# A Fourier branch whose channel transform moves from the tiles to once per unit (8 cores, Trainium2)

## The reference, cut to what matters

```python
def fourier_branch(a, w_fmix, b_fmix):
    a4 = a.reshape(B, S, 4, 128).astype(jnp.float32)
    f = jnp.fft.fft2(a4, axes=(1, 3), norm="ortho").real.astype(a.dtype)
    y = jnp.einsum("bsgc,gcd->bsgd", f, w_fmix) + b_fmix
    return y.reshape(B, S, 512)
...
h = rmsnorm(x, norm_g) * (1.0 + scale[:, None, :]) + shift[:, None, :]
a, ga, u, v, gb, ma, mb = jnp.split(h @ w_in, IN_SPLITS, axis=-1)
y_a = fourier_branch(a, w_fmix, b_fmix) * jax.nn.silu(ga)
y_b = sgu_branch(u, v, sgu_ln_g, sgu_ln_b, w_s, b_s) * jax.nn.silu(gb)
merged = jax.nn.sigmoid(ma) * (y_a @ w_pa) + jax.nn.sigmoid(mb) * (y_b @ w_pb)
out = x + gate[:, None, :] * (merged @ w_out)      # then a final rmsnorm
```

## Time and profile before

| | |
|---|---|
| median of 3 timed runs | 1279.31 us (1278.76 to 1287.62) |
| the profiled execution's own time | 1272.01 us |
| its span, slowest core | 1270.5 us (cores 1264.0 to 1270.5) |
| granted TensorE clock, mean | 0.992 to 0.995 of full |
| busy share PE, DVE, ACT, POOL | 96%, 49%, 38%, 28% |

### The profile page before, as it was taken

How to read it: one execution, slowest core, us unless ns; L and a number is a source line. 1 busy time by engine, 2 the same in 40 slices (tenths; PEclk the granted TensorE clock), 3 DMA queues, 4 the chain that set the end, 5 groups by cost and what they waited for, 6 DMA issues and landing times.

```text
span 1270.5 us, 19981 instructions; the slowest of 8 cores (1264.0 to 1270.5 us)
## 1 busy us (share of the span) xinstructions
PE 1222.7 (96%) x6504; PEld 587.9 (46%) x6504; DVE 627.7 (49%) x945; ACT 483.2 (38%) x818; POOL 349.5 (28%) x430
## 2 busy tenths in 40 slices
PE   6798999999999999989999999999999999999997
PEld 1354454444444455545444444444444444444443
DVE  0383265364756578844435434443446444344434
ACT  1483312323423368743332333243323423333322
POOL 0221132730522332203713213213128122132121
PEclk9899999999999999999999999999999999999999
DMA  8999895234426297656312212121262112121111
GB/s 273 265 254 186 167 170 164 67 116 147 156 80 208 77 302 266 194 164 137 100 50 67 84 50 84 67 90 60 84 136 86 72 62 95 50 84 67 64 70 67
DMA packets 57331, 158.21 MB, mean 125 GB/s; under 512 B 6026, under 2 KB 18698, under 8 KB 56078
## 3 DMA queue, kind: packets, MB, share of 16 engines
q1 hardware_dynamic: 46814, 130.58, 31.2%
q0 software_dynamic: 9120, 17.96, 9.2%
q10 hardware_dynamic: 1296, 8.40, 1.9%
HBM read 143.41 MB, written 31.47 MB: 138 GB/s over the span
## 4 chain that ended last, share of the span: by engine, by line
PE 84%; DMA 8%; DVE 2%; POOL 2%; issue 2%; ACT 1%; ACTq 0%; SPq 0%; DVEq 0%; POOLq 0%
PE ps L680 42%; PE ps L607 13%; PE ps L490 6%; PE ps L778 6%; PE ps L772 6%; PE ps L690 5%; PE ps L447 3%; DMA arena<-w_ada 2%; DMA arena<-Gd 2%; DMA arena<-w_out 2%; DMA arena<-xA 1%; POOL arena L783 1%; POOL arena L675 1%; DMA Gd<-arena 1%; PE ps L500 1%
## 5 line engine op out<-in xcount | busy, mean ns | idle before, releaser
L680 PE MATMUL ps<-arena 128*128 128x512 bf16 x2688 | 602.6, 380 | 2.4 <-DVE arena L729 1.7
L680 PEld LDWEIGHTS ps<-arena 128*128 128x128 bf16 x2688 | 262.1, 98 | 318.3 <-issue 8.0
L764 ACT ACTIVATE arena<-ps 128x512 bf16<-128x512 f32 x192 | 113.2, 596 | 282.8 <-PE ps L680 257.6
L783 POOL TENSOR_TENSOR arena<-arena 128x512 bf16<-128x512 bf16 x84 | 116.3, 1384 | 248.5 <-DVE arena L781 248.5
L775 DVE TENSOR_TENSOR arena<-ps,arena 128x512 bf16<-128x512 f32 x96 | 66.3, 691 | 223.1 <-PE ps L772 223.1
L607 PE MATMUL ps<-arena 128*128 128x512 bf16 x768 | 171.3, 379 | 4.0 <-DVE arena L783 1.5
L408 POOL TENSOR_TENSOR stat<-stat,eps_sb 128x1 f32<-128x1 f32 (+1 forms) x114 | 29.2, 256 | 380.9 <-ACT arena L615 298.6
L612 DVE TENSOR_TENSOR arena<-ps,arena 128x512 f32<-128x512 f32 x96 | 66.0, 691 | 126.8 <-PE ps L607 126.8
L607 PEld LDWEIGHTS ps<-arena 128*128 128x128 bf16 x768 | 74.6, 98 | 93.2 <-issue 5.5
L427 DVE TENSOR_SCALAR arena<-arena,stat 128x1024 bf16<-128x1024 f32 x96 | 81.6, 876 | 60.1 <-POOL stat L410 59.8
L421 ACT ACTIVATE arena<-arena 128x1024 bf16<-128x1024 f32 x96 | 101.2, 1054 | 22.9 <-DMA arena<-xA 16.9
(11 more groups left out here) (80 smaller groups left out, 936.9 us busy)
## 6 DMA issues: line engine op xcount, KB each, us to landing
arena<-xB SPq DMA_DIRECT2D x96, 512.0 KB, 4.4
arena<-xA SPq DMA_DIRECT2D x48, 512.0 KB, 6.3
yu<-arena SPq DMA_DIRECT2D x48, 512.0 KB, 2.8
arena<-w_ada SPq DMA_DIRECT2D x24, 512.0 KB, 5.6
arena<-w_in POOLq DMA_DIRECT2D x9, 1024.0 KB, 17.9
arena<-w_ada ACTq DMA_DIRECT2D x8, 1024.0 KB, 23.7
Gd<-arena SPq DMA_DIRECT2D x48, 128.0 KB, 5.0
arena<-Gd SPq DMA_DIRECT2D x12, 512.0 KB, 8.1
```

What stands on the lines that cost most here:

```text
L680: S.pe([lambda e, kc=kc: e.matmul(ps[b][:], lhsT=w_in_sb[:, sec, kc, col:col + 128], rhs=tb.hT[:, kc, :], start=(kc == 0), stop=(kc == 7)) ...
L764: S.op("act", lambda e, b=b, so=so: e.activation(out=bv(so, 512), in_=ps[b][:], func=AF.Sigmoid), reads=[("ps", b)], writes=gk(so, 1024))
L783: S.op("pool" if dmc < 7 else "dve", lambda e: e.tensor_tensor(out=tb.mg[:, dmc, :], in0=tb.mg[:, dmc, :], in1=bv(sl[1], 512), op=ALU.add) ...
```

## The change

`csw` loses its third part (-S). The new `z_tr(uz, g)` multiplies all 1056 columns of the real part of a group with C and of the imaginary part with S, in six matmuls of 352 columns, and evicts each in place, over the spectrum, as bf16, on ScalarE and VectorE in turn. `fourier_gate` takes the place of `fourier_out`: it has no matmul; VectorE forms sum and difference of the two transformed parts in f32 in `O_TYB`, and then adds the bias and multiplies.

The places: for unit 0 the transform is ahead of the pair's `u_section`; tile 0's gates come between the two u sections and tile 1's in the first four steps of tile 0's merge loop. For unit 1 the transform is in tile 4 after the GA section, that tile's gates after its u section. For unit 2 it is in tile 5, a group after each of the four sections. In tiles 2, 3 and 5 to 11 the gates are emitted between the GA section and the u section.

```diff
-            S.op("act", lambda e, g=g, b=b: e.activation(out=csw[:, g, 2, :], in_=ps[b][:, 128:256], func=AF.Copy, scale=-1.0),
...
+    def z_tr(uz, g):
+        for r in range(2):
+            zr = Zv[:, uz, g, r].rearrange("p s w -> p (s w)")
+            for c in range(3):
+                b = newbank()
+                zc = zr[:, c * 352:(c + 1) * 352]
+                S.pe([lambda e, b=b, zc=zc, r=r: e.matmul(ps[b][:, 0:352], lhsT=csw[:, g, r, :], rhs=zc, start=True, stop=True)],
+                     reads=[("z", g, uz), ("csw", g)], writes=[("ps", b)])
+                evict(zc, ps[b][:, 0:352], [("ps", b)], [("zq", g, uz, r, c)])
+
+    def fourier_gate(tb, u, t, g):
         uz = (1, 0, 1)[u]
         s0, s1 = 4 * t, (4 * t + 8) % 16
...
+        tf = fv(O_TYB, 512)
+        tv = tf.rearrange("p (s h w) -> p s h w", s=4, h=2)
+        rk = [("z", g, uz)] + [("zq", g, uz, r, c) for r in range(2) for c in range(3)]
+        for h, sl, w0, op in ((0, s0, 0, ALU.add), (1, s1, 2, ALU.subtract)):
+            S.op("dve", lambda e, h=h, sl=sl, w0=w0, op=op: e.tensor_tensor(
+                out=tv[:, :, h, :], in0=Zv[:, uz, g, 0, sl:sl + 4, w0:w0 + 64], in1=Zv[:, uz, g, 1, sl:sl + 4, w0:w0 + 64], op=op),
+                reads=rk + ["tyf"], writes=[("tyh", h)] + (gk(O_TYB, 2048) if h == 0 else []))
+        v = tb.sga[:, g, :]
+        sk = gk(tb.a + 1024 * g, 1024)
+        S.op("dve", lambda e: e.scalar_tensor_tensor(out=v, in0=tf, scalar=bfm_sb[:, g:g + 1], in1=v, op0=ALU.add, op1=ALU.mult),
+             reads=gk(O_TYB, 2048) + [("tyh", 0), ("tyh", 1), "tab2"] + sk, writes=sk + gk(O_TYB, 2048) + ["tyf"])
...
+    for g in range(4):
+        z_tr(1, g)
+    u_section(T0)
+    for g in range(4):
+        fourier_gate(T0, 0, 0, g)
+    u_section(TB1)
     for tb in pair:
-        u_section(tb)
-    for i, tb in enumerate(pair):
         sgu(tb)
-        fourier_out(tb, 0, i)
...
+        if dmc < 4:
+            fourier_gate(TB1, 0, 1, dmc)
...
         def after(sec):
             finish()
+            if T == 5:
+                z_tr(1, sec)
...
         after(2)
+        if T == 4:
+            for g in range(4):
+                z_tr(0, g)
+        else:
+            for g in range(4):
+                fourier_gate(tb, u, t, g)
         u_section(tb)
         after(3)
+        if T == 4:
+            for g in range(4):
+                fourier_gate(tb, u, t, g)
...
         sgu(tb)
-        fourier_out(tb, u, t)
```

More of the change, by code:

```diff
@@ L203 @@
 O_CSW = O_FG + 4096
-O_F = O_CSW + 3072
+O_F = O_CSW + 2048
 O_WST = O_F + 512
@@ L322, in build_nc @@
     fg_bc = fv(O_FG, 1024)
-    csw = bv(O_CSW, 1536).rearrange("p (g v d) -> p g v d", g=4, v=3)
+    csw = bv(O_CSW, 1024).rearrange("p (g v d) -> p g v d", g=4, v=2)
     F_sb = bv(O_F, 128)
@@ L385, in channel_tables @@
                  reads=["tab2"] + ck, writes=[("ps", b)])
-            S.op("act", lambda e, g=g, b=b: e.activation(out=csw[:, g, 0:2, :].rearrange("p v d -> p (v d)"), in_=ps[b][:, 0:256], func=AF.Copy),
-                 reads=[("ps", b)], writes=[("csw", g)])
-            S.op("act", lambda e, g=g, b=b: e.activation(out=csw[:, g, 2, :], in_=ps[b][:, 128:256], func=AF.Copy, scale=-1.0),
+            S.op("act", lambda e, g=g, b=b: e.activation(out=csw[:, g].rearrange("p v d -> p (v d)"), in_=ps[b][:, 0:256], func=AF.Copy),
                  reads=[("ps", b)], writes=[("csw", g)])
@@ L735, in sgu @@
                  reads=gk(to, 1024) + sk, writes=sk)
-    def fourier_out(tb, u, t):
+    def z_tr(uz, g):
[7 more added lines that the diff above has]
+                evict(zc, ps[b][:, 0:352], [("ps", b)], [("zq", g, uz, r, c)])
```

## The result

| | before | after |
|---|---|---|
| median of all four executions, same chip | 1283.46 us | 1315.36 us |
| the three that the ratio uses | 1278.76 to 1287.62 us | 1310.38 to 1315.61 us |
| ratio of the times | | 1.025, 95% interval 1.0215 to 1.0284 |
| span of core 7 | 1270.5 us | 1303.7 us |
| TensorE matmuls | 6504 | 6384 |

What follows compares the result with a forecast made beforehand. TensorE's queue of matmuls, almost without holes, was taken as the bound. Saved columns and new waits summed to +23.9 us, with +5 for the clock +29: 1308 us against the median of 1279.3, range 1287 to 1322.

Steps and rivals of the forecast that it cites:

- rival (c): TensorE's clock: each of the new waits drops it to half, +23.9 + 15 = 1318 us; chance 0.16.
- parts 1 and 2: TensorE: 192 removed matmuls save 20.9 us, 72 added ones of 352 columns cost 10.7; columns save 10.2.
- part 3: VectorE: a gate of two sums and one scale-and-multiply takes 1.71 us, four 6.84 in the place of 2.72.
- rival (a): Waits between VectorE operations are free: four gates take 5.4 us; 1290 without half clock, 1293 with some; chance 0.12.
- part 4: Gates ahead of u evictions eat a steady tile's saving; second merge product waits: +0.6 us, six tiles +3.6.
- Tile 3: Three accumulations run before the gates; merge gates start 2.55 us later, second merge product adds 0.55: +3.1.
- Tile 2: out_chunk between u and SGU gives cover: merge gates 2.4 us earlier, second merge product waits about 1.7: -0.7.
- Tile 4: Transform bound by evictions, +5.2 us; gates after u make the second merge product wait 3.7; in all +7.9.
- Tile 5: Transform groups after each section wait for PSUM banks, behind v and behind u: +10.9 us, 3.6 of it matmuls.
- The pair: First two tiles: merge gates start at 173.3 for 174.20, -0.9 us; the second tile's gates cost 0.
- part 8: Half clock behind some of the new waits: 0 to +15 us, taken as about a third, +5.
- Rival (b): TensorE's columns decide, if four gates fit in 4.6 us and the transform's matmuls are hidden: -10.2, 1269 us; chance 0.10.

Runs made afterwards that it cites:

- bf16_sum: The changed kernel with the gates' scratch in bf16 in the place of f32; ratio 1.0161 to the kernel before, a tile 87.19 us.
- own_bf16_two: The changed kernel with the gates' sums in bf16, in two scratches of their own in turn; ratio 1.0063 to the kernel before, a tile 85.56 us.
- z_in_merge: The changed kernel with tile 5's transform moved from behind its four sections into its merge loop's first four steps; ratio 1.0196 to the kernel before.

## Why the prediction was right

The forecast was 1308 us, +2.3%; measured +2.5%. On the spans it was +29 of 1270.5; core 7 gained 33.2. The mechanism is the forecast one, tile by tile, but two things should be called by their names. That the waits sum to 24.3 for 23.9 is partly luck: the start and tile 2 came out 3.6 dearer than forecast, tiles 3, 4, 5 and the steady ones 3.2 cheaper. And by the total alone, 1315, rival (c) with its 1318 is nearer than the forecast; what decides against it is where the clock fell, not the time. By the steps:

- **Columns** (parts 1 and 2). TensorE's price of a 352-column matmul was interpolated at 0.149 and is 0.89 / 6 = 0.148. A tile without waits is 85.56, 2.06 less than before, where 1.74 are the removed matmuls, 0.16 the old wait, and the rest small gaps.
- **A gate** (part 3). 1.71 predicted (the terms as written sum to 1.70), 1.72 measured; 0.42 + 0.42 - 0.08 = 0.76 for the pair of sums is what the timeline shows, and 0.10 stand between an operation and the one that reads it (789.74 to 789.84). So rival (a) is out. The Trainium skill's rule in VectorE: DVE Perf Modes, section The DRAIN you can't avoid, that a semaphore after each of a chain of copies costs nothing extra, doesn't carry over to this chain. A gate of bf16_sum waits for the one before and starts 0.1 us after its end; a gate of own_bf16_two doesn't and starts 0.08 before it (771.04 + 0.75 - 771.71). Their gates take 1.45 and 1.33.
- **Steady tile** (part 4). A wait of 2 us at the merge gates, predicted and measured (1.93), a short one at the second merge product, 0.6 predicted and 0.45 measured. Tile +0.63 for +0.6. Tile 8 is the exception: before it took 89.4, 1.8 more than its neighbours, since the load of w_out came 52.3 us after v's first matmul, and after 88.4, so there the lateness fell into a wait that was there already, and the six tiles came to +2.2 and not +3.6.
- **Tile 3.** The wait of 4.60 (4.40 on cores 1 to 5) was 4.45 by the prediction (2.55 later, plus the 1.74 of matmuls gone and the 0.16 before).
- **Tile 2**, the first miss. The merge gates were right (42.3 us after v for 44.7 before: -2.4). The wait at the second merge product was to be 1.7 and was 2.70, since GpSimd's four products took 5.46 for 4.49, and half clock followed (1.7): +2.2 for -0.7.
- **Tile 4.** Transform 5.2 predicted, 4.79 and a wait of 0.38 measured; last wait 3.7 predicted, 3.71 measured. Without clock +6.7 for +7.9: the groups of `s3_joint` ahead of the transform ended 33.4 us after v's first matmul for 35.0 before, of which 1.4 are three short waits of before (0.39, 0.37, 0.67) that didn't come back. I had taken that stretch as fixed.
- **Tile 5.** +10.7 without clock for +10.9. Waits of 3.41 and 0.35 us stand behind ScalarE's writing of the normalised v (L699), 2.22 and the short ones behind u. z_in_merge shows it from the other side: 9.5 us come back when only the place of the transform changes.
- **The pair**, the second miss. The merge gates came 29.50 us after GA's first matmul for 29.85 before, which looks like -0.35 for -0.9. But before, half clock stood inside this stretch and cost 1.7; now short waits (0.52, three of 0.2 and 0.38) push it behind the stretch, onto the merge gates:

```profile
174.01 8.75 PE L678 MATMUL ps<-arena 128*128 128x512 bf16 x32 [0.38 <-DVE arena L727]
```

  They take 1.7 more than before. At full clock the pair thus lost 1.3 us and didn't gain 0.9: the -0.9 came from a full-clock sum set against a time of before that had the half clock in it. The +1.5 at the start of tile 2 is -0.6 ahead of the first v section, +0.8 up to GA of the second tile, -0.35 and +1.7. The first two are within what cores of one run differ by there (269.0 to 278.6 us at the start of tile 2).
- **The clock** (part 8), the term that was mis-sized: 5 predicted, 8.9 measured from tile 2 on (and the 1.7 of the pair, which the kernel before paid as well). I had taken a third of the waits; on core 7 it was every wait of 2.6 us and more from tile 2 on and the cluster of 2.22, 0.29, 0.29, 0.21 and 1.24 in tile 5, and none of the steady tiles' (1.93 five times, 2.28 in tile 7). Rival (c), every new wait, was to give +15 and is out for that reason. A fixed number could not have been right: behind the same wait of 2.70 in tile 2 the clock fell on core 7 and stayed full on core 1.
- **Rival (b)** needed four gates in 4.6 us. No f32 version comes near; own_bf16_two reaches the point by starting 1.5 us earlier and taking 5.4, and then the tile is at its bound.

What stays open: why cores 0 to 3 had stretches at 0.81 in the profiled run of the changed kernel. Cores 0 and 1 have them within 0.3 us of each other, and so have cores 2 and 3, though the cores' tiles don't start together; on core 1 no wait of over 0.2 us stands in the 8 us ahead of them, but for the second. No experiment was made on them.

## What to carry to other kernels

When a product on the bound engine is turned into work for an idle engine, the price isn't its busy time but what stands behind it in that engine's queue: the same four gates cost 8 to 9.5 us a tile behind SGU, 2.7 ahead of u, and nothing between the silu groups. Before placing them, write down for each candidate place which bank the queue's next operation frees and when the bound engine asks for it. And count the first occurrence, the last, and the tile with another order apart: here two of twelve tiles made more than half of the loss.

## What the hardware did that I hadn't expected

- **The same wait is followed by half clock or not.** On core 7 after the change, 1.93 (five times) and 2.28 us of idle were followed by a clock of 1.00; 2.62, 2.70, 3.41, 3.71 and 4.60 by 0.50 for 3 us and more, a price of 1.5 to 2.4 us on top of the wait. That looks like a step, but it isn't one: before the change, waits of 2.46, 2.60 and 2.74 on the same core were followed by full clock, and on core 4 one of 2.24 by half clock. I counted TensorE's waits in all twelve profiles, from 70 us on, where the clock was full before (without the cores on which records of matmuls are missing). Half clock began during the wait or within 3.5 us of its end for 5 of the 89 waits of 1.85 to 2.2 us, for 72 of the 126 of 2.2 to 3.4, and for all 226 that were longer. In between, a forecast of such a kernel needs a range for the clock and not a number.
- **GpSimd and VectorE slow each other when each reads two inputs from SBUF.** GpSimd's four products took 5.46 us beside L619 and 4.49 alone; a pair of sums took 1.92 beside a product and 0.76 alone, 1.16 more, which is one product (4.49 / 4 = 1.12). The Trainium skill says so in SBUF — State Buffer, section SBUF: two separate sides: a VectorE operation with two SBUF inputs and a GpSimd operation that reads SBUF exclude each other for a whole instruction. These runs agree with it. It fits that a scratch of its own gained nothing behind SGU: the wait of 1.47 us for GpSimd went, and the sums beside GpSimd's product took 1.16 more.
